# Head sums in column strips, spread in row strips, and new step orders on three engines

## The reference, cut to what matters

```
kk = k * k_k
kk = kk / max(sqrt(sum(kk * kk over the head's 64 channels)), 1e-12)
... state recurrence over the tokens gives y ...
m = mean(y over the head);  var = mean((y - m)^2 over the head)
y = (y - m) * rsqrt(var + 64e-5) * ln_w + ln_b
```

## Time and profile before

| | |
|---|---|
| median of 3 runs (lowest to highest) | 470.05 us (469.38 to 470.31) |
| the profiled execution | 471.19 us, span 469.4 us, mean granted clock 0.994 |
| PE matmul busy | 453.8 us, 97% of the span, 4470 matmul instructions |
| DVE, ACT busy | 322.0 us (69%), 236.5 us (50%) |
| POOL busy in tenths, 40 slices | 8200000000000000072000001340000000000000 |
| DMA | 73.05 MB, 156 GB/s |
| fetches of the program (queue q8) | 35 packets, 0.57 MB |

### The profile page before, as it was taken

How to read it: one execution, slowest core, us unless ns; L and a number is a source line. 1 busy time by engine, 2 the same in 40 slices (tenths; PEclk the granted TensorE clock), 3 DMA queues, 4 the chain that set the end, 5 groups by cost and what they waited for, 6 DMA issues and landing times.

```text
span 469.4 us, 10481 instructions
## 1 busy us (share of the span) xinstructions
PE 453.8 (97%) x4470; PEld 411.1 (88%) x4470; DVE 322.0 (69%) x487; ACT 236.5 (50%) x373; POOL 35.2 (8%) x51
## 2 busy tenths in 40 slices
PE   4999999989999999999999999999999999999994
PEld 4999999989899879999998898888888888888883
DVE  4689999896485557668766367876556656574746
ACT  5799843342444426436544355545464545454534
POOL 8200000000000000072000001340000000000000
PEclk9999999989999999999999999999999999999998
DMA  7964534605051442372552165655546565756502
GB/s 245 338 212 130 180 113 150 191 3 182 3 170 39 139 133 89 123 236 90 180 181 89 27 191 183 227 182 179 179 145 214 184 194 169 249 187 218 190 0 89
DMA packets 60385, 73.05 MB, mean 156 GB/s; under 512 B 1314, under 2 KB 49524, under 8 KB 60340
## 3 DMA queue, kind: packets, MB, share of 16 engines
q1 hardware_dynamic: 60260, 72.14, 48.0%
q0 software_dynamic: 80, 0.26, 0.1%
HBM read 71.35 MB, written 1.05 MB: 154 GB/s over the span
## 4 chain that ended last, share of the span: by engine, by line
PE 92%; DVE 3%; DMA 1%; ACT 1%; issue 1%; SPq 0%; ACTq 0%
PE bank L534 13%; PE bank L549 11%; PE bank L550 10%; PE bank L551 10%; PE bank L566 6%; PE bank L568 6%; PE bank L567 6%; PE bank L536 6%; PE bank L917 2%; PE bank L502 2%; PE bank L503 1%; PE bank L504 1%; DMA xval<-in_x 1%; PE bank L941 1%; PE bank L488 1%; PE bank L533 1%
## 5 line engine op out<-in xcount | busy, mean ns | idle before, releaser
L1622 DVE TENSOR_TENSOR w_lo<-raw,w_hi 128x1024 fp32r<-128x1024 f32 x130 | 160.2, 1239 | 68.5 <-ACT w_hi L1114 68.3
L1114 ACT ACTIVATE w_hi<-raw 128x1024 fp32r<-128x1024 f32 x130 | 136.8, 1057 | 111.4 <-PE bank L551 51.0
L534 PE MATMUL bank<-op,w_hi 128*128 128x512 f32 x256 | 89.1, 398 | 0.0
L549 PE MATMUL bank<-op,w_hi 128*128 128x256 f32 x288 | 83.7, 291 | 0.1
L550 PE MATMUL bank<-op,w_hi 128*128 128x256 f32 x288 | 81.4, 283 | 0.0
L551 PE MATMUL bank<-op,w_lo 128*128 128x256 f32 x288 | 81.4, 283 | 0.0
L536 PE MATMUL bank<-op,w_lo 128*128 128x256 f32 x224 | 62.8, 280 | 0.0
L549 PEld LDWEIGHTS bank<-op,w_hi 128*128 128x128 f32 x288 | 55.1, 191 | 1.0 <-issue 0.6
L550 PEld LDWEIGHTS bank<-op,w_hi 128*128 128x128 f32 x288 | 55.2, 192 | 0.2
L551 PEld LDWEIGHTS bank<-op,w_lo 128*128 128x128 f32 x288 | 55.1, 191 | 0.0
L534 PEld LDWEIGHTS bank<-op,w_hi 128*128 128x128 f32 x256 | 46.4, 188 | 8.8
(11 more groups left out here) (275 smaller groups left out, 715.1 us busy)
## 6 DMA issues: line engine op xcount, KB each, us to landing
raw<-in_w_ff SPq DMA_DIRECT2D x32, 1024.0 KB, 5.3
raw<-in_w_in SPq DMA_DIRECT2D x12, 1024.0 KB, 5.5
raw<-in_w_xkv SPq DMA_DIRECT2D x8, 1024.0 KB, 5.5
raw<-in_w_mix_out SPq DMA_DIRECT2D x4, 1024.0 KB, 4.9
raw<-in_w_xq SPq DMA_DIRECT2D x4, 1024.0 KB, 5.0
raw<-in_w_xo SPq DMA_DIRECT2D x4, 1024.0 KB, 5.7
xval<-in_x SPq DMA_DIRECT2D x2, 512.0 KB, 4.8
raw<-in_w_in SPq DMA_DIRECT2D x2, 512.0 KB, 5.8
```

What stands on the lines that cost most here:

```text
L534: last = mm(b[:, :], wh[:, k, :], op_both[0][:, :, k, :], start=first, stop=final)
L549: mm(dst, wh[:, k, :], op_hi[which][:, k, :], start=first, stop=False)
L1114: op(view(w_hi), r, ACT.Copy).then_inc(hi_done, 1)
L1622: tt(view(w_lo), r, view(w_hi).bitcast(f32), ALU.subtract).then_inc(lo_done, 1)
```

## The change

The head sums get the indicator as the stationary operand, now 32 columns wide (two used, 30 zero), and the squares of 256 tokens as the moving one. The four p go to four strips of 32 output partitions of bank 0, so hsum is 128 x 256: in partitions 32p and 32p+1 the two heads of tile p, tokens in the columns. Root and reciprocal work on that. For the spread a second indicator, `sel`, has in rows 32p and 32p+1 ones for the 64 channels of each head; four matmuls, each on a strip of 32 rows, write to four banks, 0 to 3. The copy to 64 columns is gone, and `hwide` with it.

```diff
-        ind = sb("ind", [128, 2])
+        ind = sb("ind", [128, 32])
+        sel = sb("sel", [128, 128])
-        hsum = sb("hsum", [128, NT * NH])
-        hwide = AR[:, 2:4, :, :, :].rearrange("p a n b t -> p (a n b t)")
+        hsum = sb("hsum", [128, T])
...
             def head_sums(src, signal):
-                for n in range(NT):
-                    for p in range(NP):
-                        c = NH * n + 2 * p
-                        last = mm(B[0][:, c:c + 2], src[:, p, tokens_of(n)], ind[:, :], start=True, stop=True)
+                for p in range(NP):
+                    last = mm(B[0][32 * p:32 * p + 32, 0:T], ind[:, :], src[:, p, :], start=True, stop=True)
                 last.then_inc(signal, 1)
-            def spread_heads(banks, signal):
+            def spread_heads(signal):
                 for p in range(NP):
-                    for n in range(NT):
-                        c = NH * n + 2 * p
-                        o = (p % 2) * T + 128 * n
-                        last = turn_op(B[banks[p // 2]][:, o:o + 128],
-                                       hwide[:, HD * c:HD * c + 128], ident[:, :])
+                    r = slice(32 * p, 32 * p + 32)
+                    last = mm(B[p][:, 0:T], sel[r, :], hsum[r, :], start=True, stop=True)
                 last.then_inc(signal, 1)
...
             def gate():
                 pe.wait_ge(gate_in, 16)
+                pe.wait_ge(dve_norm, 1)
...
-            def widen(signal):
-                link(nc.vector.reciprocal(hsum[:, :], hsum[:, :]))
-                cp(hwide.rearrange("p (h k) -> p h k", k=HD),
-                   hsum[:, :].unsqueeze(2).to_broadcast([128, NT * NH, HD])).then_inc(signal, 1)
+            def invert(signal):
+                nc.vector.reciprocal(hsum[:, :], hsum[:, :]).then_inc(signal, 1)
             def key_norm():
                 dve.wait_ge(pe_kk, 1)
-                ts(hsum[:, :], B[0][:, 0:NT * NH], 1e-24, None, ALU.max).then_inc(dve_kk, 1)
+                ts(hsum[:, :], B[0][:, 0:T], 1e-24, None, ALU.max).then_inc(dve_kk, 1)
```

More of the change, by code:

```diff
@@ L998, in _ @@
             solve(3)
-            dense(3)
+            dense(2)
             outq(0, 0)
             pair_flip(0)
+            dense(1)
+            pair_values(0)
             outq(0, 1)
             outq(0, 2)
[L1004 to L1007, removed]
             outq(0, 3)
             outq(1, 0)
+            dense(5)
+            pair_scores(1)
             outq(1, 1)
             outq(1, 2)
+            outq(1, 3)
             dense(2)
[L1013 to L1016, removed]
             phi(0)
@@ L1019, in _ @@
             phi(1)
-            dense(2)
-            pair_scores(2)
+            pair_flip(1)
+            dense(1)
+            pair_values(1)
             psi(0, 0)
@@ L1024, in _ @@
             psi(0, 2)
-            dense(1)
             psi(0, 3)
+            pair_scores(2)
+            dense(2)
             psi(1, 0)
@@ L1031, in _ @@
             dense(1)
-            pair_flip(2)
             state(1)
-            dense(1)
+            dense(2)
             state(2)
-            pair_values(2)
             dense(1)
             state(3)
-            dense(1)
+            pair_flip(2)
             state(4)
             dense(1)
+            pair_values(2)
             state(5)
@@ L1060, in _ @@
             scores(0)
-            dense(4)
+            dense(3)
             turn(0)
@@ L1428, in _ @@
             hi(37)
+            pair_flip(2)
+            pair_values(2)
             hi(38)
+            pair_scores(3)
             deviation()
-            pair_scores(3)
             deviation_root()
@@ L1460, in _ @@
             hi(56)
+            turn(0)
             hi(57)
-            turn(0)
             scores(1)
-            hi(58)
             values(0)
             turn(1)
+            hi(58)
+            scores(2)
             hi(59)
-            scores(2)
             values(1)
@@ L1496, in _ @@
             hi(72)
-            follow(34)
+            follow(33)
             part(2, 0)
@@ L1501, in _ @@
             hi(74)
+            follow(34)
+            hi(75)
+            part(3, 0)
             follow(35)
-            part(3, 0)
-            hi(75)
+            hi(76)
+            hi(77)
             part(3, 1)
-            hi(76)
-            follow(36)
-            hi(77)
             hi(78)
@@ L1541, in _ @@
             hi(96)
+            hi(97)
             part(8, 0)
-            hi(97)
             part(8, 1)
             hi(98)
+            hi(99)
+            follow(40)
+            part(9, 0)
+            hi(100)
             follow(41)
-            part(9, 0)
-            hi(99)
+            hi(101)
             part(9, 1)
-            residual(1)
-            hi(100)
-            follow(42)
-            hi(101)
             hi(102)
@@ L1559, in _ @@
             part(10, 1)
-            residual(2)
-            residual(3)
             hi(106)
+            part(11, 0)
+            follow(42)
+            hi(107)
             follow(43)
-            part(11, 0)
-            hi(107)
             part(11, 1)
             hi(108)
-            follow(44)
             hi(109)
@@ L1601, in _ @@
             hi(129)
+            residual(2)
+            residual(3)
             finish()
@@ L2187, in _ @@
             lo(46)
+            take(22)
             lo(47)
-            take(22)
             lo(48)
@@ L2226, in _ @@
             lo(61)
+            lo(62)
             take(29)
-            lo(62)
             lo(63)
@@ L2232, in _ @@
             lo(64)
+            take(31)
             lo(65)
@@ L2235, in _ @@
             follow(30)
-            take(31)
             lo(67)
+            take(32)
             follow(31)
-            take(32)
+            follow(32)
             lo(68)
-            follow(32)
             add(0, 0)
@@ L2246, in _ @@
             lo(70)
-            hidden(0)
             add(1, 0)
@@ L2361, in _ @@
             lo(124)
+            hidden(14)
+            lo(125)
             hidden(15)
-            lo(125)
             lo(126)
```

414 lines of the change are left out of this document (207 added, 207 removed).

## The result

The changed kernel takes 473.46 us (median of 6 runs, 472.0 to 474.05), the kernel before beside it 470.18 (6 runs, 469.2 to 471.23). The ratio is 1.0061, 95% interval 1.0043 to 1.008. I had forecast 468.1 us and a range up to 470.8: the sign is wrong.

A forecast was written before the change was run, and what follows sets the result against it. PE (97% busy) was taken as the bound, with DVE also full from 38 to 67 us. Terms summed to -1.9 us: 471.19 to 469.3 profiled, 468.1 on the runs' scale; 8-in-10 range 465.2 to 470.8.

The forecast's parts named there:

- the term of the program packets: At pair_values(0), moved ahead of the outq bursts, the stop for issue goes: -0.7 us, bounds -0.7 and +1.5.
- two more such stops: Stops for issue like pair_values(0)'s, in the new order's bursts: +1.4 us in the rival, +1.5 as the term's bound.
- packets move: Rival: at the outq and psi bursts, the old stop's gain fails and two more come: 470.2 us, chance 0.11.
- Head sums and spreads: On PE, both places: sums 0.67 us each, saving 1.1 and 1.0; spreads 0.67 us each, counted as 0.
- DVE's part: Longer reciprocal and maximum at the head sums: 1.05 us more on DVE; PE waits about 0.5 us before tokens.
- The first place: First head sum, in DVE's full stretch: PE's 1.1 us gain goes to a wait before tokens, net +0.3 us.
- the second place: Second head sum: DVE has slack there, so nothing is paid and PE gains 1.0 us.
- Start: Spread(0) moves behind two more quarters, leaving its old slot idle: +0.4 us, bounds 0 and 0.5.
- The wait at 222 us: A dense matmul that needs lo(51), which DVE now does one step earlier: -0.2 us.
- Groups: PE's groups of small work between dense stretches fall from 48 to 43: -0.8 us, bounds 0 and -1.3.
- The join: At join (L751), PE's 1.6 us wait for DVE and the slow clock behind it stay: 0.
- Slower by DVE and the clock: Rival, 38 to 75 us: DVE slips 1.8 us more, the clock halves for 1.6 more: 471.5 us, chance 0.13.

The follow-up runs named there:

- e2: The kernel before's functions (old arithmetic) with the three new engine orders and the wait that bonus needs for them: 468.68 us, ratio 0.9952 to the kernel before.
- e5: The changed kernel with two weight loads (issued at 104.75 and 122.2 us) held back by waits on SP: 466.9 us, ratio 0.9916 to the kernel before.
- e1: The new functions (head sums, spreads, reciprocals, two added waits) with the three engine orders of the kernel before: 470.26 us against 470.54, ratio 0.9993.
- e6: Control: the kernel before with the same two weight loads held back: 470.63 us, ratio 1.0001 to the unaltered kernel before.
- e8: The changed kernel with only the second weight load (122.2 us) held back, to the end of the outq steps' first half: 470.45 us, ratio 0.9981 to the kernel before.

## Why the prediction was wrong

**The step that failed is the term of the program packets.** I had the mechanism in hand (the unexplained 0.35 us of issue, fetches of 256 instructions) and sized it wrongly, in three ways. I took the stop as the property of one place and wrote -0.7 for moving that place out of the bursts, instead of counting 256 instructions at a time along the new list, which could have shown packets of 3.8 and 3.3 us. I took "two more such stops" as 1.4 us at most, each of the size of the earlier trace rows, whose fetch ran on quiet engines; behind a weight load they are 2.21 and 1.60. And I hung no clock on them, though the earlier trace rows shows what a stop can bring: 2.3 us more. For the -0.7 of the sum the traces show +3.5 (stops of 3.81 us for the 0.35 of the earlier trace rows), and the clock besides. The rival "packets move" was the right one, with 470.2 for 473.5 and a chance of 0.11. Undoing the stops by two waits on SP moves the changed kernel by 6.6 us (473.46 to 466.9), to 0.9916 of the kernel before, where the forecast was 0.996: the other terms together were better than I had taken them, and the stops hid that.

I also weighed a rule there that would have set the term to 0. "Runtime: NRT & Kernel Launch", Instruction fetch mechanics, of the Trainium skill says that an engine's program is fetched in blocks of 256 instructions, the next while the current one runs, and that the cost of crossing into a new block is mostly hidden. The blocks agree with these traces; hidden holds for dense work, and not for packets of small matmuls, which lost up to 3.36 us at one crossing.

The other terms, in the prediction's order:

*Head sums and spreads*: right. Eight instructions take 0.64 us (0.67 taken), the spreads 0.71:

```profile
...
42.14 0.64 PE L663 MATMUL bank<-s,ind 128*32 128x256 f32 x8
...
46.23 0.71 PE L670 MATMUL bank<-hsum,sel 32*128 32x256 f32 x8
...
178.99 0.64 PE L663 MATMUL bank<-s,ind 128*32 128x256 f32 x8
...
```

*DVE's part*: its durations are right (the two rows below, by line, answer), DVE is busy for 28.89 of the 29 us, and PE waits before tokens where I had said, for a shorter time (0.27 us by its matmul, 0.47 by its weight load, for L1823 at 67.5; about 0.5 foretold). The first place was still a gain and not +0.3, the second term that was mis-sized, and the other way: from e2 to e5, two kernels almost without stops that differ by the arithmetic and the loads, quarter 6 starts 0.20 us earlier, quarter 19, behind the head sum, 1.25, and quarter 40, past the tokens, still 1.17. So the wait before the tokens did not eat the head sum's 1.1 us. At the second place quarter 74, right behind the head sum, gains another 1.02, as forecast (1.0).

```profile
...
L1776 DVE RECIPROCAL hsum<-hsum 128x256 f32<-128x256 f32 x2 | 3.5, 1750 | 0.0
...
L1780 DVE TENSOR_SCALAR hsum<-bank 128x256 f32<-128x256 f32 x1 | 0.4, 419 | 0.0
...
```

*Start*: +0.4 taken. From quarter 0 to quarter 6 the changed kernel takes 10.98 us and the kernel before 10.55, so 0.43 more; but single traces scatter here (e2 10.83, e5 10.67; e1, with the old order, 10.31). *The wait at 222 us* is gone, and the feed-forward part is neutral, as taken.

*Groups*: -0.8 can't be read by itself. The orders alone (e2) gave 1.9 us with the old stops gone; the terms that belong to them, -0.8, -0.7, -0.2, +0.4 and +0.1, make -1.2. The half clock behind the join, which e2's trace lacks, accounts for 1.6 in the trace of the kernel before, so it can't be told what of the 1.9 the orders themselves gave.

*The join*: its wait stayed (1.4 for 1.6), the half clock behind it, which I had taken to stay, did not. Nor is it a fixed price of that wait: in e1 and e6, which have the old order, the same wait of 1.64 and 1.63 us has a clock of 1.00 in all of the 4.7 us behind it. My price "from a stop of about 1.6 us on the clock halves" rested on one trace and does not hold.

*Slower by DVE and the clock*, the rival that I gave the other sign, had the right sign by the wrong road: its place was 38 to 75 us, and there the longest wait of PE's matmuls for DVE is 0.35 us.

## What to carry to other kernels

Where an engine runs bursts of short instructions, count its program in packets of 256 and compare each packet's length with the fetch (here 3 to 4 us, 5 to 7 behind a large load); "issue" inside a run of equal instructions is the sign to look for. A large load issued just ahead of such an edge is best held back until the burst is through, and idle time at the start is room for a few instructions that shift all edges. A small, innocent edit shifts them too, so two kernels that differ by 16 instructions can differ by 6 us for no reason of their own.

## What the hardware showed unexpectedly

The program's fetch shares the DMA engines with the weights and waits behind them: in the packets of the table it began 0.4 to 1.7 us after its edge without weights ahead of it and up to 4.05 us after it with them. The clock does not follow from a stop's length alone: it stayed at 1.00 behind stops of 1.58 and 2.21 us in the changed kernel and fell to 0.50 behind one of 1.60; behind the join stop of e8, 2.48 us long, the mean was 0.71; and behind the wait of 1.6 us before the join it fell to 0.50 in the kernel before and stayed at 1.00 in e1 and e6. What decides it stays open. Four column strips over all 128 rows do run side by side, eight passes of 256 columns in 0.64 us, where eight in turn took 1.73 (L678).
